# Four transposes of the previous round moved ahead of the round's fourth projection on TensorE, in a streaming encoder layer

## What is computed

```python
h = rmsnorm(x, norm_g)
proj = h @ w_in                       # 1024 -> 2832 columns
aq, ak, av, ag, gq, gk, gv, gg, glr, cv, cgl, cg = jnp.split(proj, offsets, axis=-1)
# group 1: windowed attention on aq, ak, av, gated by ag
# group 2: gated linear attention on gq, gk, gv, glr, gated by gg
# group 3, the convolution group (256 channels):
u = cv * jax.nn.sigmoid(cgl)
c = depthwise_conv(concat([conv_hist, u]), conv_w, width=31) + conv_b
c = jax.nn.silu(layernorm(c, ln_g, ln_b)) @ w_pw + b_pw
y_conv = c * jax.nn.silu(cg)
y = concat([y_attn, y_gla, y_conv], axis=-1) @ w_out
return x + y, ...                     # and the new windows and states
```

## Time and profile before

| what | value |
|---|---|
| time, median of 3 runs | 1076.29 us (1072.7 to 1079.73) |
| time of the profiled execution | 1079.73 us |
| its span, first to last instruction | 1078.0 us |
| mean granted TensorE clock | 0.945 of full speed |
| TensorE busy | 974.3 us |
| VectorE busy | 770.9 us |
| ScalarE busy | 468.2 us |
| GpSimd busy | 181.4 us |

### The profile page before, as it was taken

One profiled execution on the slowest core, in us unless ns is written; L12 is line 12 of the kernel. 1 busy time (PEld: TensorE's weight loads), 2 busy tenths in 40 slices (PEclk: granted clock), 3 DMA queues, 4 the chain that ended last, 5 costly groups with the idle time before them and its releaser, 6 DMA issues.

```text
span 1078.0 us, 15970 instructions
## 1 busy us (share of the span) xinstructions
PE 974.3 (90%) x5835; PEld 848.8 (79%) x5835; DVE 770.9 (72%) x1864; ACT 468.2 (43%) x1131; POOL 181.4 (17%) x216
## 2 busy tenths in 40 slices
PE   6769999999999999995549688999999999999956
PEld 4657888888888888884349577898989898999944
DVE  6477777777777777766545865778888787878872
ACT  7366666666666666656443203224141515041400
POOL 0321222222222222110001121011111212121210
PEclk9979999999999999996769778999999999999987
DMA  9512222222222222312740110212111111212021
GB/s 306 184 60 107 92 95 100 98 96 91 90 91 94 98 98 79 104 62 69 194 134 3 39 42 1 88 51 69 50 59 60 59 60 49 69 40 79 1 81 39
DMA packets 57437, 88.37 MB, mean 82 GB/s; under 512 B 9648, under 2 KB 33968, under 8 KB 57360
## 3 DMA queue, kind: packets, MB, share of 16 engines
q1 hardware_dynamic: 57360, 87.36, 24.5%
HBM read 60.80 MB, written 26.60 MB: 81 GB/s over the span
## 4 chain that ended last, share of the span: by engine, by line
PE 83%; DVE 9%; DMA 3%; ACT 3%; issue 1%; POOL 1%; SPq 1%; DVEq 0%; ACTq 0%; POOLq 0%
PE J L1749 21%; PE J L611 20%; PE J L1778 9%; PE J L626 8%; PE J L1763 5%; PE T L1683 3%; PE S L1693 3%; PE S L1655 3%; PE T L1628 2%; DVE acc L1323 2%; PE T L1827 1%; DMA wraw<-in_w_in 1%; DVE wlo L452 1%; PE S L1895 1%; PE T L1879 1%
## 5 line engine op out<-in xcount | busy, mean ns | idle before, releaser
L1323 DVE SCALAR_TENSOR_TENSOR acc<-ub,cwh,acc 128x256 f32<-128x256 f32 (+1 forms) x480 | 221.0, 525 | 0.3
L1749 PE MATMUL J<-xbh,whi 128*128 128x256 f32 (+1 forms) x512 | 152.0, 297 | 23.8 <-DVE xbl L504 23.8
L611 PE MATMUL J<-whi,xhi 128*128 128x512 f32 (+1 forms) x408 | 150.3, 368 | 10.4 <-DVE wlo L452 10.4
L1749 PE MATMUL J<-xbl,whi 128*128 128x256 f32 (+1 forms) x512 | 148.2, 289 | 0.0
L1749 PE MATMUL J<-xbh,wlo 128*128 128x256 f32 (+1 forms) x512 | 148.1, 289 | 0.0
L611 PE MATMUL J<-wlo,xhi 128*128 128x512 f32 (+1 forms) x408 | 146.7, 360 | 0.0
L611 PE MATMUL J<-whi,xlo 128*128 128x512 f32 (+1 forms) x408 | 146.6, 359 | 0.0
L1749 PEld LDWEIGHTS J<-xbh,whi 128*128 128x128 f32 x512 | 99.3, 194 | 27.1 <-issue 26.6
L1749 PEld LDWEIGHTS J<-xbl,whi 128*128 128x128 f32 x512 | 99.3, 194 | 0.2
L1749 PEld LDWEIGHTS J<-xbh,wlo 128*128 128x128 f32 x512 | 98.9, 193 | 0.0
L611 PEld LDWEIGHTS J<-whi,xhi 128*128 128x128 f32 x408 | 78.0, 191 | 21.8 <-DVE xlo L586 10.0
(11 more groups left out here) (229 smaller groups left out, 2200.7 us busy)
## 6 DMA issues: line engine op xcount, KB each, us to landing
out<-res SPq DMA_DIRECT2D x64, 256.0 KB, 2.0
x_normed_scratch<-xraw SPq DMA_DIRECT2D x17, 512.0 KB, 2.9
xraw<-xT SPq DMA_DIRECT2D x16, 512.0 KB, 3.5
xtok<-in_x_prompt SPq DMA_DIRECT2D x16, 512.0 KB, 5.0
res<-in_x_prompt SPq DMA_DIRECT2D x16, 512.0 KB, 5.6
xbraw<-x_normed_scratch SPq DMA_DIRECT2D x16, 512.0 KB, 4.8
res<-out SPq DMA_DIRECT2D x16, 512.0 KB, 4.1
wraw<-in_w_in SPq DMA_DIRECT2D x52, 128.0 KB, 2.5
```

The source lines that it names most:

```text
L611: last = nc.tensor.matmul(bank[:, 0:width], x[x_slot(ps, t)][:, k, :], w, start=(k == 0 and n == 0), stop=(k == KT - 1 and n == 2))
L1323: nc.vector.scalar_tensor_tensor(acc[:, j, 0:frames], src, w, acc[:, j, 0:frames], ALU.mult, ALU.add).then_inc(conv_step, 1)
L1749: last = nc.tensor.matmul(bank[:, 0:w], wt, x[:, k, 0:w], start=(k == 0 and m == 0), stop=(k == KT - 1 and m == 2))
```

## The change

In rounds 1 to 7 `conv_T` for the pair of prompt tiles is issued before `project_b("cv", b, 1)`, and not after it. Rounds 0 and 8 have only one of the two pieces and stay as they are.

```diff
                     project_b("cgl", b, 0)
                     project_b("cv", b, 0)
                     project_b("cgl", b, 1)
-                    project_b("cv", b, 1)
                 for g in done:
                     if g[3] != (2,):
                         conv_T(g)
+                if cur:
+                    project_b("cv", b, 1)
                 for g in done:
                     o_T(g)
```

## The result

| kernel | median of four runs | lowest to highest |
|---|---|---|
| before | 1076.1 us | 1072.7 to 1079.73 |
| changed | 1089.53 us | 1088.0 to 1092.16 |

The changed kernel takes 1.0127 times as long (95% interval 1.0088 to 1.0166), 13.4 us more by the medians. The profiled execution of the changed kernel took 1088.83 us. The forecast was 1090.2 us, in a range of 1085 to 1102 us.

A forecast was written before the change was run, and what follows sets the result against it. TensorE was taken to bound rounds 2 to 7. Their pauses, 11.5 us, plus 2.4 us for round 1 gave 13.9 us, forecast as 1090.2 us on the median's scale, in a range of 1085 to 1102 us.

The forecast's parts named there:

- TensorE as the bound of rounds 2 to 7: Rounds 2 to 7: TensorE has no idle time, so each microsecond it stands idle there is added to the time.
- The steady rounds: Rounds 2 to 7: TensorE waits at the transposes for VectorE's taps; 1.85 us in round 2, 1.93 each in 3 to 7.
- The pause doesn't shrink: Rounds 2 to 7: the taps hang on the same round's project_b("cv", b, 0), so VectorE's lead is worth 0.08 us at most.
- Round 1, 2.4 us: Round 1: a 4.2 us wait before the transposes, project_b("cv", b, 1) probably at half clock, part regained; 2.4 us net.
- VectorE's waits: Rounds 2 to 7: the wait before L1372 drops from 1.74 to about 0.5 us; about 2 us appears before the second glu.
- The clock as a rival: Rounds 2 to 7: the clock falls in each pause, 2.25 us more a round, 13.5 us, 1103.7 us in all; chance 0.25.
- The lead that is kept: Rounds 2 to 7: VectorE keeps its gain, the pause shrinks to nothing after round 3; 5.3 us, 1081.6 us; chance 0.06.
- the wait that isn't there: At the transposes: the taps are complete when TensorE arrives, so the time stays at 1076.3 us; chance 0.01.

The follow-up runs named there:

- The run with a pause of 4.47 us: Against the changed kernel, the transposes stand one projection earlier still, ahead of both project_b("cgl", b, 1) and project_b("cv", b, 1): 1121.48 us, ratio 1.0408.
- measured alone: The change made in rounds 2 to 7 only, round 1 in the old order, against the kernel before: 1088.42 us, ratio 1.0110.
- 2.3 us (0.6 to 3.9) alone: The change made in round 1 only, rounds 2 to 7 in the old order, against the kernel before: 1079.26 us, ratio 1.0021.
- 12 matmuls in front: Against the kernel before, the transposes are issued inside project_b("cv", b, 1), behind 12 of its 24 matmuls: 1076.68 us, ratio 1.0000.
- 18 of 24 matmuls in front: Against the kernel before, the transposes are issued inside project_b("cv", b, 1), behind 18 of its 24 matmuls: 1073.88 us, ratio 0.9974.

## Why the prediction was right

**TensorE as the bound of rounds 2 to 7.** Right. A pause of 1.64 us came through in full, with 0.2 us for the restart behind it. The run with a pause of 4.47 us shows the same at more than twice the size.

**The steady rounds, 1.93 us each and 11.5 us in all.** Right: 1.87 us in each round in the profile, 11.2 us, and 11.8 us (9.4 to 14.4) when measured alone. The small difference lies in the step from the released transposes to cv1's first matmul. It was taken from round 1 as 0.49 us (636.68 to 637.17) and is 0.41 us here (769.23 to 769.64).

**The pause doesn't shrink.** Right. All six waits are 1.6 us. The reason given was that the taps hang on cv0 of the same round, and the chain after shows just this path.

**Round 1, 2.4 us.** The size agrees within what can be told: 2.3 us (0.6 to 3.9) alone. The steps agree in the profile of the change: a pause of 4.0 us (forecast 4.2), cv1 at half speed in 5.07 us (5.1), `project_v` 4.4 us later against the end of the taps (4.4) and then at full speed, so that it ended only 2.2 us later (2.2). One step was too short: the transposes took 0.77 us at the low clock (634.51 to 635.28), not 0.49. What the prediction didn't have is that round 1 as a whole varies more than its 2.4 us from one execution to the next: 76.35 and 79.5 us with the old order, and 79.4 to 80.8 us with the new one, whose pause was 3.23, 4.00 and 4.23 us in three profiles. That 2.4 us came so close to the measured 2.3 is in part luck.

**VectorE's waits.** Forecast: 0.5 us before the statistics and 2 us before the second glu; measured: 0.75 and 1.80 us.

**The clock as a rival.** It did not fall in any of the 18 steady rounds of the three profiles that have the change there, at a pause of 1.6 us followed by transposes. The rule of the Trainium skill that was named for it ("TensorE: Matmul & The Clock Gate", section "Part 4: PE-mode transpose") says that a transpose doesn't count as busy time of TensorE in the same way as a matmul. By it the pause and the transposes are one stand of some 2.0 us, and even so the clock stayed at 1.00. No run here tells whether transposes count. The price set for a fall was somewhat high: 2.25 us were forecast and about 1.7 us found a round with the pause of 4.47 us.

**The lead that is kept, and the wait that isn't there.** Both wrong, as forecast with small chances: the waits didn't shrink, and the operand was late.

**What stays open.** The kernels with the transposes inside cv1 are 2.8 us faster than before or level with it where 0.3 to 3.3 us slower was expected, and it is not in rounds 2 to 7. In their profiles the clock didn't fall at 639 us as it did before. Over the profiles, round 1 took 75.7 to 76.6 us in the five without that fall and 79.0 to 80.8 us in the five with it (the run with two projections behind the transposes, 83.4 us, left out), so the fall goes with some 3 us. The old order in round 1 also ran once without the fall (76.35 us). The clocks of all executions point the same way for 12 matmuls in front. Whether the order itself makes the fall rarer was not shown.

## What to carry to other kernels

When an instruction is moved forward on the engine that bounds the kernel, first look up when its operand is complete. If it is complete only after the new place is reached, the difference is a pause, and on an engine that has no idle time elsewhere in the round, as here, it was paid in full in every round, whatever it gave to the other engines. Here the operand was 1.1 us early in the old place and 1.7 us late in the new one, and the order of a few matmuls decided between them. Work that has no such operand belongs between the two, and it need not be whole groups: 18 of 24 matmuls in front were enough, and the split cost 0.01 us a round at most.

## What the runs showed of the hardware that was not expected

GpSimd's addition of 128x8 elements took 2.28 us beside four taps of 350 columns on VectorE, 7.21 us beside 14 of them, and 0.38 us in rounds 2 to 8, where the taps have 256 columns, also with 14 of them in a row. In round 1 it ended 0.05 to 0.08 us after the last tap, with four taps as with 14. The Trainium skill ("GPSIMD Engine Reference", section "1. Specifications") names a contention of GpSimd with VectorE instructions that have two SBUF inputs. Round 1 agrees with that. The steady rounds, whose taps have the same two inputs from SBUF, don't show it, and no run here tells the two apart.
